# Closing a feed-forward network: the last squares of the last piece summed by TensorE, and another pace for the normalisation around them

## The reference

```python
def rms_norm(x, w):
    y = xf * lax.rsqrt(jnp.mean(xf * xf, axis=-1, keepdims=True) + EPS)
    return (y * w.astype(jnp.float32)).astype(x.dtype)
...
    h = h + (silu(u @ w_ffn_gate) * (u @ w_ffn_up)) @ w_ffn_down     # feed-forward 1 (f0)
    x = rms_norm(h, norm_final_w)                                    # "double": two norms in a row
    xn = modulate(rmsnorm(x, norm_mix[0]), shift, scale)             # xn * (1 + scale) + shift
    # differential attention, then feed-forward 2 (f1) over tokens and context
    xn, xc = modulate(rmsnorm(h, norm_mix[1]), ...), modulate(rmsnorm(hc, norm_mix[1]), ...)   # "mod"
    # neighbourhood attention, then feed-forward 3 (f2)
    return rmsnorm(h, norm_final)                                    # "final"
```

## Time and profile before

| what | value |
|---|---|
| median of 3 runs | 2755.51 us (2754.37 to 2759.36) |
| the profiled execution | 2757.04 us |
| its span on the core | 2755.1 us, mean granted TensorE clock 0.971 |
| TensorE busy | 2569.0 us, 93% of the span |
| VectorE busy | 1531.8 us, 56% |
| ScalarE busy | 1096.7 us, 40% |
| GpSimd busy | 321.7 us, 12% |
| sums of squares on GpSimd (L2090) | 63 instructions, 50.1 us |

### The profile page before, as it was taken

How to read it: one execution, slowest core, us unless ns; L and a number is a source line. 1 busy time by engine, 2 the same in 40 slices (tenths; PEclk the granted TensorE clock), 3 DMA queues, 4 the chain that set the end, 5 groups by cost and what they waited for, 6 DMA issues and landing times.

```text
span 2755.1 us, 36972 instructions
## 1 busy us (share of the span) xinstructions
PE 2569.0 (93%) x14795; PEld 2198.5 (80%) x14795; DVE 1531.8 (56%) x2878; ACT 1096.7 (40%) x1928; POOL 321.7 (12%) x199
## 2 busy tenths in 40 slices
PE   7988889999997999998899999999899998999998
PEld 6787777878886877776788888888788787777877
DVE  3565547657747777677745443436455556533334
ACT  5544534222234655555521211114566556422222
POOL 2222100000012222121000000002223222000001
PEclk9999999999998999999899999999999999999999
DMA  4111033535521111111233333330323222222231
GB/s 118 47 39 51 19 107 122 176 124 181 169 84 47 39 39 39 31 39 39 69 100 123 104 110 113 103 123 24 73 52 73 52 53 60 73 96 86 96 108 47
DMA packets 247333, 223.86 MB, mean 81 GB/s; under 512 B 36916, under 2 KB 215898, under 8 KB 247162
## 3 DMA queue, kind: packets, MB, share of 16 engines
q1 hardware_dynamic: 247162, 221.49, 26.8%
HBM read 219.24 MB, written 2.22 MB: 80 GB/s over the span
## 4 chain that ended last, share of the span: by engine, by line
PE 77%; DVE 11%; ACT 7%; issue 4%; POOL 0%; DMA 0%; SPq 0%; DVEq 0%; POOLq 0%; ACTq 0%
PE ps L363 24%; PE ps L365 22%; PE ps L364 22%; DVE FR L527 2%; ACT FR L522 1%; PE ps L2815 1%; ACT whi L388 1%; PE ps L652 1%; PE ps L1071 1%; PE ps L2401 1%; ACT FA L2494 1%; PE ps L2826 1%; DVE hT L2574 1%; DVE FA L2614 1%; DVE raw L1444 1%
## 5 line engine op out<-in xcount | busy, mean ns | idle before, releaser
L363 PE MATMUL ps<-Uh,whi 128*128 128x512 f32 (+2 forms) x2544 | 904.2, 355 | 25.2 <-ACT FA L2513 5.9
L364 PE MATMUL ps<-Ul,whi 128*128 128x512 f32 (+2 forms) x2544 | 888.3, 349 | 0.0
L365 PE MATMUL ps<-Uh,wlo 128*128 128x512 f32 (+2 forms) x2544 | 887.8, 349 | 0.0
L363 PEld LDWEIGHTS ps<-Uh,whi 128*128 128x128 f32 x2544 | 491.2, 193 | 97.1 <-issue 20.0
L365 PEld LDWEIGHTS ps<-Uh,wlo 128*128 128x128 f32 x2544 | 489.7, 193 | 60.4
L364 PEld LDWEIGHTS ps<-Ul,whi 128*128 128x128 f32 x2544 | 491.2, 193 | 57.7
L388 ACT ACTIVATE whi<-raw 128x1024 fp32r<-128x1024 f32 (+2 forms) x205 | 296.4, 1446 | 555.0 <-PE ps L365 554.8
L399 DVE TENSOR_TENSOR wlo<-raw,whi 128x2048 fp32r<-128x2048 f32 (+2 forms) x121 | 248.3, 2053 | 299.3 <-ACT whi L388 299.1
L363 PE MATMUL ps<-FR,whi 128*128 128x512 f32 (+1 forms) x864 | 305.6, 354 | 24.9 <-DVE FR L527 20.1
L364 PE MATMUL ps<-FR,whi 128*128 128x512 f32 (+1 forms) x864 | 302.2, 350 | 0.0
L365 PE MATMUL ps<-FR,wlo 128*128 128x512 f32 (+1 forms) x864 | 301.8, 349 | 0.0
(11 more groups left out here) (334 smaller groups left out, 3289.0 us busy)
## 6 DMA issues: line engine op xcount, KB each, us to landing
FA<-in_ada_w_dram SPq DMA_DIRECT2D x192, 256.0 KB, 2.8
raw<-in_ffn_w_gate_up_dram SPq DMA_DIRECT2D x44, 1024.0 KB, 5.1
raw<-in_ffn_w_down_dram SPq DMA_DIRECT2D x24, 768.0 KB, 4.3
raw<-in_w_in_dram SPq DMA_DIRECT2D x29, 512.0 KB, 3.9
raw<-in_da_wqkv_dram SPq DMA_DIRECT2D x24, 512.0 KB, 3.7
raw<-in_na_wqkv_dram SPq DMA_DIRECT2D x24, 512.0 KB, 3.8
raw<-in_w_ffn_gate_dram SPq DMA_DIRECT2D x11, 1024.0 KB, 5.3
raw<-in_w_ffn_up_dram SPq DMA_DIRECT2D x11, 1024.0 KB, 5.4
```

Source lines behind the costliest of these rows:

```text
L363: e.matmul(out, ah, bh, start=start, stop=False)
L364: e.matmul(out, ah, bl, start=False, stop=False)
L365: return e.matmul(out, al, bh, start=False, stop=stop)
```

## The change

For the last piece of each close, GpSimd's last additions are left out: blocks 6 and 7 in "double" (of both sums), block 7 in "mod" and "final". TensorE instead does a product of ones with the accumulator and then one with each remaining square straight from its buffer in `st_sq4`, all into the same PSUM bank; it waits for GpSimd's last remaining sum and then for each square. GpSimd's instructions go from 63 to 57, the float32 products with ones (of two passes each) from 9 to 15. `tail_place` tells TensorE's program which buffer a square is in.

```diff
--- before.py
+++ after.py
@@ -231,6 +231,7 @@
         self.used = {}
         self.lo_by = {}
         self.xbank = {}
+        self.tail_place = {}
         self.ada_bank = {}
         self.layout()
 
@@ -1894,7 +1895,7 @@
 
 def tail_after(f, engine):
 
-    start, pace = {"double": (5.0, 1.0), "mod": (1.6, 1.0), "final": (1.6, 0.55)}[f.kind]
+    start, pace = {"double": (5.0, 1.45), "mod": (1.6, 1.45), "final": (1.6, 0.55)}[f.kind]
     blocks = range(KC)
     if engine == "scalar":
         ones = [("root", 0.1)] + [("second", 3.0)] * (f.kind == "double") + [(("hi", c), start + 0.5 + pace * c) for c in blocks if f.kind != "final"]
@@ -1906,10 +1907,26 @@
         if f.kind != "final":
             ones += [(("lo", c), start + 1.0 + pace * c) for c in blocks]
         if f.kind == "double":
-            ones += [(("keep", c), start + 9.0 + 0.5 * c) for c in blocks]
+            ones += [(("keep", c), start + 12.6 + 0.5 * c) for c in blocks]
         return {"open": (("open", 0.0),), "split": (("split", 0.5),), "split_last": (("split", 2.2),), "tail": (("add", 0.1),), "ada_end": (("ada_end", 0.1),),
                 "ones": ones, "turn": (("turn", 0.1),)}
     return {"tail": (("sum", 1.0),)}
+
+
+def tail_summed(f, i):
+
+    return KC if i < len(f.pieces) - 1 else KC - 2 if f.kind == "double" else KC - 1
+
+
+def tail_sum_tensor(K, e, w, f, o, i, z):
+
+    p, n = f.pieces[i], tail_summed(f, i)
+    w.wait_ge(*K.at("pool_sum", f.st, n - 1, i, z))
+    t = e.matmul(o, K.ones[:, :], (K.st_acc, K.st_acc2)[z][:, p.t0:p.t1], start=True, stop=n == KC)
+    for m in range(n, KC):
+        w.wait_ge(*K.at("square", f.st, m, i, z))
+        t = e.matmul(o, K.ones[:, :], K.st_sq4[:, K.tail_place.get((f.st, m, i, z), 0), :], start=False, stop=m == KC - 1)
+    return t
 
 
 def tail_tensor(K, e, w, f):
@@ -1936,13 +1953,11 @@
         elif what == "ones":
             p = f.pieces[i]
             o = K.hold(w, i, ("norm_ln", f.after, i))[:, 0:256]
-            w.wait_ge(*K.at("pool_sum", st, KC - 1, i, 0))
-            t = e.matmul(o, K.ones[:, :], K.st_acc[:, p.t0:p.t1], start=True, stop=True)
+            t = tail_sum_tensor(K, e, w, f, o, i, 0)
             if f.kind == "double":
                 t.then_inc(*K.ev("norm_sum", f.after, i, 0))
                 o = K.hold(w, 3, ("norm_mid", f.after, i))[:, 0:256]
-                w.wait_ge(*K.at("pool_sum", st, KC - 1, i, 1))
-                t = e.matmul(o, K.ones[:, :], K.st_acc2[:, p.t0:p.t1], start=True, stop=True)
+                t = tail_sum_tensor(K, e, w, f, o, i, 1)
             t.then_inc(*K.ev("norm_sum", f.after, i))
         elif what == "turn":
             w.wait_ge(*K.at("y_scaled", KC - 1, i))
@@ -1967,6 +1982,7 @@
         if len(K.tail_sq) >= 4:
             w.wait_ge(*K.at("pool_sum", *K.tail_sq[-4]))
         K.tail_sq.append((f.st, n, i, z))
+        K.tail_place[f.st, n, i, z] = k
     e.activation(out, K.hT[:, n, p.t0:p.t1], ACT.Square, scale=scale).then_inc(*K.ev("square", f.st, n, i, z))
 
 
@@ -2081,7 +2097,7 @@
         p = f.pieces[i]
         for z in range(2 if f.kind == "double" else 1):
             acc = (K.st_acc, K.st_acc2)[z][:, p.t0:p.t1]
-            if n:
+            if 0 < n < tail_summed(f, i):
                 k = len(K.tail_sq) % 4
                 K.tail_sq.append(n)
                 w.wait_ge(*K.at("square", f.st, n, i, z))
```

## The result

| kernel | median us (runs) | ratio to before, 95% interval |
|---|---|---|
| before | 2754.51 (20) | |
| changed | 2761.93 (20) | 1.0025 (1.0017 to 1.0032) |

What follows compares the result with a forecast made beforehand. TensorE carries 77% of the chain that ended last, so changes count where it waits. Mod +8.8, double +1.1, final -0.9 give +9.0 us: 2766.0, less 1.5 for a median, 2764.5; range 2759 to 2770.5.

Steps and rivals of the forecast that it cites:

- first rival: VectorE and GpSimd don't collide, so mask additions behind mod block nothing: +4.0 us in all, 2759.5; chance 0.12.
- The order of VectorE and the price of a tile: In mod, each low half waits directly behind its scaled instruction (1.05 us); a tile costs VectorE 1.94 us against TensorE's 1.44.
- Mod's last addition: VectorE's last addition in mod comes 4.1 us later (bounds +2.8, +5.9), 7 us behind TensorE's last tile.
- The bank that tile 7 needs late: In mod, the PSUM bank for tile 7 comes late; counted only in the +5.9 us upper bound.
- Mod, behind the last addition: From mod's last addition to the second projection's end: late low halves and blocking mask additions, +4.7 us (bounds +1.0, +7.5).
- third rival: Longer waits in mod and two projections keep TensorE at 1.2 GHz longer: about 4 us more, 2768.5; chance 0.14.
- Double: The double close, to the end of its keep block: +1.1 us later (bounds -0.9 and +2).
- removed waits there are worth 0.85 at most: In double's stage from 840 on, VectorE is 19.15 of 20 us busy, so removed waits gain 0.85 us at most.
- The bare pairs and later halves: In double, the last piece's bare pairs take 1.45 us instead of 0.91, +1.6, plus two waits behind the root.
- Final: The final close: the sum between last square and product goes, -0.9 us (bounds -0.7 and -1.0).
- Second rival: No bare wait if low follows scaled within 0.64 us in the closes: mod -3.5, total -4.9, 2750.6; chance 0.08.
- The sign that the wait of mod's product: In the profile after, mod's product waits longer than 5.1 us and is released by ScalarE, not GpSimd.

Runs made afterwards that it cites:

- Run 3: Changed kernel with low halves due at start + 1.5 + pace x c instead of 1.0, so scaled c+1 precedes low c; 2752.32 us, ratio 0.9993.
- Run 1: Changed kernel with the old due times (pace 1.0, keep at 9.0), only the last squares going into the product; 2750.4 us, ratio 0.9978.
- run 4: Changed kernel with GpSimd's first mask addition behind mod waiting for the close's last low half; 2764.04 us, ratio 1.0037.
- run 6: Changed kernel with double at pace 1.45, low due at start + 1.5, and mod at pace 1.0, low at start + 1.0; 2749.79 us, ratio 0.9980.

## Why the prediction was right

The time, 2764.5 forecast and 2761.93 measured, came out by the mechanism that was forecast; most steps were a little too dear, +9.0 us in all against +7.9 by the stages and +6.9 by the whole times. The first rival's 2759.5 lies within the stated range as well, so it is the steps that tell the two apart, not the range. The range was also said to take in all bounds of mod and double; at its lower end it doesn't (2.8 + 1.0 - 0.9 - 0.9 is +2.0, 2757.5).

- **The order of VectorE and the price of a tile.** 1.94 forecast, 1.94 measured in mod's middle piece, with 1.05 from scaled to low half. Run 3 shows that this is the cause: with one instruction between them the last addition comes 6.3 us earlier, of which only 0.4 can be put down to the one instruction fewer (7 instead of 8) that then stands ahead of it.
- **Mod's last addition**, +4.1 forecast, +3.90 measured, 6.35 us behind TensorE's last tile (3.1 before; the sign said 7). The root comes 1.0 us sooner behind it, as forecast: 2.23 us against 3.23. The bank that tile 7 needs late cost TensorE one gap of 0.4 us, hidden by the wait that follows.
- **Mod, behind the last addition**, +4.7 forecast, +4.35 measured (8.25 - 3.90). VectorE set the pace: the last block of the second projection waits 0.70 us for the last low half. The mask additions began 12.6 us behind the last addition (12.5 forecast). They held one instruction for 2.33 and one for 1.71 us. I had them block low 4 and scaled 5; by then VectorE was one instruction further, and they held it in 3.1 of the 4.6 us only ((2.33 - 0.48) + (1.71 - 0.48)).
- **The lower clock** (third rival). In both kernels a stretch of 6.8 us begins while TensorE still waits for the product (1922.1 before, 1921.4 now). Now there is a second one of 6.8 us from 1931.7. So what this rival named did occur: between the product and the split the granted clock was at its lower level for 11.1 us, against 5.8 before. The second stretch cost nothing up to the split, since TensorE was through with all but the last block of the second projection 0.70 us before VectorE had low 7 of the last piece ready. That was not in the forecast's reasoning, and no run changes the clock alone.
- **Double**, +1.1 forecast, +0.54 measured. The step that was mis-sized is "removed waits there are worth 0.85 at most". Run 1 shows 2.05 for the removed sums. The 0.85 is the idle time of the window from 840 on. Just ahead of that window lie VectorE's wait of 1.31 us for the high half behind the root (it ends at 839.71), on which the end of the stage hung, and the 1.4 us that GpSimd held VectorE, though I had named the blocking for mod. About 0.5 of the 2.05 is the product's clock (run 1). The bare pairs and later halves then cost 2.6 (29.11 - 26.52), not about 2.
- **Final**, -0.9 forecast, -0.85 measured.
- **First rival** (no collision). Its +4.0 is outside the interval, and run 4 shows the collision directly. I had taken its removal to be worth 3.3 us in that run; it was worth 2.1 at the split, 0.7 at the transposes and nothing that shows in the whole, since the same 4.3 us meet other work.
- **Second rival** (faster). Its limit, 0.64 us from scaled to low half, was missed in every tile. But its picture of an early last addition being a gain of 3.5 was wrong too: run 3 had that addition at 18.41 and mod didn't gain, since late low halves then took the product's place, and 6.8 us at the lower clock came with them.
- The sign that the wait of mod's product would be "released by ScalarE, not GpSimd" was wrong in its first half: the accumulator's product waited for GpSimd's sum of block 6 (6.20 us), and the last square's followed without a gap in the list. In final the release was ScalarE's. Of the two instructions that the mask additions held, the one over 2 us was a scaled one, not a low half.

The Trainium skill, SBUF — State Buffer, section "SBUF: two separate sides", has VectorE and GpSimd lock a shared port pair. The traces agree: a scaled or low instruction, which reads two SBUF operands, takes 2.3 to 2.4 us where it first meets a mask addition of about 2.2 us (before, changed, runs 1, 3 and 6) and 0.48 or 0.49 in run 4, where the mask additions start later. Additions of tiles, which read one operand in PSUM, are at 0.41 to 0.48 throughout, also beside a sum (834.82 in the earlier trace rows, with GpSimd at work from 830.40 on in the earlier trace rows).

## What to carry to other kernels

When a planner's due times interleave two chains on an in-order engine, compare not only how many instructions stand ahead of the urgent one but which of them wait: a dependent pair that goes through another engine needs at least one independent instruction between its halves (here 1.05 us instead of 0.40 for the second one). Moving work behind the urgent instruction only helps as far as its consumer can wait; here pace 1.2 was better than both 1.0 and 1.45, by mod's stage to the split. And a part that gains may be hidden in a change that loses: the last squares were worth 4.5 us by the stages and 3 to 9 by whole times, and the due times took more than that back.

## What the runs showed of the hardware that I had not expected

VectorE's busy time contains time in which it is only held by GpSimd. In double, five instructions took 3.79 us beside GpSimd's sums and 2.37 without them (run 1), so there it had more room than its idle time says. What made the stage 2.05 us shorter was the earlier root; the room let VectorE follow it. A window that starts a little late, like the one from 840 on with 19.15 of 20 us busy, shows neither. GpSimd is held as well: in mod a sum of squares takes 0.72 to 0.74 us where VectorE is idle beside it and 0.85 to 0.95 among VectorE's scaled and low instructions, 1.47 to 1.6 beside a weight split. And equal work of TensorE differed by 1.6 us between executions through where a 3.4 us stretch of the lower clock fell; stages measured from event to event agreed to 0.02 us where no such stretch lay in them (26.52 and 26.53; 10.61, 10.60 and 10.61).
